# Six split slots and four raw slots for expert weights, splits up to five chunks ahead, and five smaller moves

## The chip, the cores and the metric
The kernel runs on one core of a Trainium2 chip. The metric is the device time of one execution in microseconds. TensorE (PE) multiplies; VectorE (DVE), ScalarE (ACT) and GpSimd (POOL) work beside it, and DMA queues issued by SyncE (SP) and GpSimd carry data between HBM and SBUF.

## What is computed
Two blocks on 256 tokens of width 1024: a mixer of three branches (attention, gated linear attention, mLSTM) and a feed-forward part, dense in the first block and a mixture of eight experts, two per token, in the second. All is float32.

```python
    for l in range(DEPTH):
        h = rmsnorm(x, attn_norm_g[l])
        x = x + hybrid_mixer(h, w_in[l], b_in[l], mlstm_conv_w[l], mlstm_conv_b[l], gla_gate_w[l],
                             gla_gate_b[l], gla_norm_g[l], w_up_moba[l], w_up_gla[l], w_up_mlstm[l], w_o[l])
        h = rmsnorm(x, ffn_norm_g[l])
        j = l // 2
        if l % 2 == 0:
            x = x + swiglu(h, ffn_w_gate[j], ffn_w_up[j], ffn_w_down[j])
        else:
            x = x + moe_swiglu(h, router_w[j], router_b[j], moe_w_gate[j], moe_w_up[j], moe_w_down[j])
    return rmsnorm(x, final_norm_g)
...
def swiglu(x, w_gate, w_up, w_down):
    return (jax.nn.silu(x @ w_gate) * (x @ w_up)) @ w_down
```

`DEPTH` is 2 and the hidden width 2816. In `moe_swiglu` each token goes to the two experts with the largest router logits, and their `swiglu` outputs are added with the softmax of the two logits as weights.

## The kernel before
**Chunks and splits.** Weights come in chunks of 128 x 2048 floats (1.05 MB), each as two DMA transfers of 512 KB that SyncE issues in order into a raw slot. A float32 product is made of three: the weights are split into a high part (a cast on ScalarE, `copy(hi_slot(m), slot_raw(m))`, L1359) and a low part (a subtraction on VectorE, L1795), and TensorE multiplies high by high, high by low and low by high. The low split increments `lo_ready`, on which TensorE waits for the chunk and SyncE for the raw slot that comes free. The dense stages do the same at L1286 and L1656.

**The expert stage** is a list MS of 8 x 33 = 264 steps, one chunk each; m is the number of a step. The hidden width is cut into 11 tiles i. Each has two gate/up chunks, `gu i c` with c = 0 and 1 (12 matmuls each, L1206), and a down chunk, `dn i` (12 matmuls, L1217). The order is gu 0, gu 1, dn 0, gu 2, dn 1 and so on; the first gate chunk of the next expert is put ahead of an expert's last down chunk. Between gate/up and down, ScalarE makes `silu` (L1586), VectorE the product `hid` (L2232), TensorE transposes it (two transposes, `rows_hidden_T`, L1184), ScalarE copies the high part (`yT_hi`, L1591) and VectorE makes the low part (`yT_lo`, L2245), which the down chunk needs. `next_hidden` says behind which step the transposes stand: before, tile i + 1 behind dn i.

**Slots.** `RE` raw slots hold loaded chunks, `RX` pairs of split slots hold the high and low parts. Before, RE = 8 and RX = 4, and step m splits chunk m + 3. The split waits for the raw data (`moe_in`) and for TensorE to be done with the slot (`slot_free`). The load of chunk m waits for the low split of chunk m - RE.

**Order.** Each engine has its own list in program order and nothing passes anything: what stands behind a waiting split on ScalarE or VectorE waits too.

**Other pieces.** At an expert pair's end (odd e, step dn 9) `gather` brings the next pair's rows onto partitions (L1135; `gather_hi` and `gather_lo`, L1546 and L2184, scale them). `rows_of_picks` (L2131 to L2139) makes row numbers in expert 0 at dn 4, `gates_of_picks` gates in expert 1 at dn 6, `gates_exp` (L1539, L1540) in expert 1 at dn 1 with two table loads. GpSimd stores normalised rows to HBM (L637), loads those of each pair from there (L644), stores each expert's output rows (L655) and at the end gathers each token's rows (L661) into `prow`, one set at a time, which VectorE adds (`add_picked`, L2147). At the very start the first chunks come as pieces (L860) and the third chunk, of which both halves count on one semaphore, is split whole.

## Time and profile before

| | |
|---|---|
| median of three runs | 1513.99 us (1512.26 to 1519.23) |
| the profiled execution | 1515.32 us, of it 1513.1 us in the span |
| TensorE busy | 1489.0 us, 98% of the span |
| VectorE, ScalarE, GpSimd busy | 1209.0, 957.2, 60.1 us |
| granted TensorE clock | 0.997 of full speed |
| DMA | 426.31 MB, 282 GB/s over the span |
| expert stage | about 742 us to 1501 us |

A busy TensorE here means that matmuls follow one another; one of 128 x 512 is shown as 0.39 us long, and the next starts 0.23 us after it. What can be won is the time in which it waits. A wait is put down to the instruction that released it last, and a wait on one engine reaches TensorE only if what stands behind it is late there.

### The profile page before, as it was taken

The numbers are of one execution on the slowest core, as the hardware profiler recorded it, in microseconds if no ns is written. First come the engines' busy times: TensorE is split into PE (matmuls) and PEld (weight loads), VectorE is DVE, ScalarE is ACT, GpSimd is POOL, SyncE is SP. The second block draws the span as 40 slices with busy tenths as digits, with TensorE's granted clock in tenths as the row PEclk, the third lists the DMA queues.
The fourth block names the chain that finished last, engine by engine and source line by source line (L and its number), as shares of the span: only waits on it lengthen the run. The fifth ranks groups of instructions, "written<-read, shape, count | busy, mean of one in ns | idle before, by whom it ended". The sixth has DMA issues, their size and how long they took to land.

```text
span 1513.1 us, 18975 instructions
## 1 busy us (share of the span) xinstructions
PE 1489.0 (98%) x7373; PEld 1239.7 (82%) x7373; DVE 1209.0 (80%) x1173; ACT 957.2 (63%) x907; POOL 60.1 (4%) x93
## 2 busy tenths in 40 slices
PE   9999999999999999999899999999999999999996
PEld 7898888888888898888788787888888888888885
DVE  6787976654556697976789899988889889889886
ACT  6357634544435357634787777777777777877774
POOL 2000000000000000001002000000000000000002
PEclk9999999999999999999999999999999999999998
DMA  8454555455545554556799999999999999999991
GB/s 337 182 178 144 201 180 182 176 193 195 185 177 197 181 187 148 189 190 256 296 370 401 410 405 363 391 373 383 379 367 388 386 378 370 350 390 380 380 375 58
DMA packets 117872, 426.31 MB, mean 282 GB/s; under 512 B 13392, under 2 KB 13568, under 8 KB 117776
## 3 DMA queue, kind: packets, MB, share of 16 engines
q1 hardware_dynamic: 111024, 402.44, 70.3%
q0 software_dynamic: 6464, 22.25, 4.2%
q8 instruction: 61, 1.00, 0.3%
q10 hardware_dynamic: 288, 0.34, 0.1%
q14 instruction: 35, 0.29, 0.1%
HBM read 415.01 MB, written 9.97 MB: 281 GB/s over the span
## 4 chain that ended last, share of the span: by engine, by line
PE 85%; DVE 5%; ACT 5%; issue 2%; DMA 1%; SPq 0%; DVEq 0%; ACTq 0%
PE ps L1206 29%; PE ps L750 17%; PE ps L1217 14%; PE ps L1049 8%; PE ps L740 4%; PE ps L1026 4%; PE ps L729 4%; DVE w_lo L1656 2%; PE ps L1184 1%; ACT w_hi L1286 1%; DVE w_lo L1795 1%; ACT hT_hi L1546 1%; DMA late<-dense_dram 1%; DMA prow<-y_rows,bias 1%; PE ps L708 1%
## 5 line engine op out<-in xcount | busy, mean ns | idle before, releaser
L1656 DVE TENSOR_TENSOR w_lo<-raw_m,w_hi 128x2048 fp32r<-128x2048 f32 x113 | 258.1, 2289 | 120.0 <-ACT w_hi L1286 120.0
L1286 ACT CAST w_hi<-raw_m 128x2048 fp32r<-128x2048 f32 x113 | 214.7, 1907 | 129.1 <-PE ps L750 59.2
L1795 DVE TENSOR_TENSOR w_lo<-raw_m,w_hi 128x2048 fp32r<-128x2048 f32 x99 | 226.5, 2291 | 24.4 <-ACT w_hi L1359 24.3
L1795 DVE TENSOR_TENSOR w_lo<-late,w_hi 128x2048 fp32r<-128x2048 f32 x99 | 226.4, 2290 | 22.4 <-ACT w_hi L1359 22.1
L1206 PE MATMUL ps<-w_hi,hT_hi 128*128 128x512 f32 x532 | 213.8, 402 | 1.3 <-DVE hT_lo L2184 1.3
L1206 PE MATMUL ps<-w_hi,hT_lo 128*128 128x512 f32 x532 | 208.8, 392 | 0.0
L1206 PE MATMUL ps<-w_lo,hT_hi 128*128 128x512 f32 x532 | 208.4, 392 | 0.0
L1359 ACT CAST w_hi<-raw_m 128x2048 fp32r<-128x2048 f32 x99 | 189.4, 1914 | 24.1 <-PE ps L1206 17.6
L1359 ACT CAST w_hi<-late 128x2048 fp32r<-128x2048 f32 x99 | 189.5, 1915 | 19.9 <-PE ps L1206 19.4
L750 PE MATMUL ps<-w_hi,hT_hi 128*128 128x512 f32 x464 | 183.5, 395 | 1.8 <-DVE w_lo L1656 1.8
L750 PE MATMUL ps<-w_hi,hT_lo 128*128 128x512 f32 x464 | 181.1, 390 | 0.0
L750 PE MATMUL ps<-w_lo,hT_hi 128*128 128x512 f32 x464 | 181.0, 390 | 0.0
L1795 DVE TENSOR_TENSOR w_lo_x<-late,w_hi_x 128x2048 fp32r<-128x2048 f32 x66 | 151.2, 2291 | 18.5 <-ACT w_hi_x L1359 18.4
L1359 ACT CAST w_hi_x<-late 128x2048 fp32r<-128x2048 f32 x66 | 126.4, 1915 | 11.7 <-PE ps L1206 11.7
L1206 PEld LDWEIGHTS ps<-w_hi,hT_lo 128*128 128x128 f32 x532 | 100.3, 188 | 21.3
L1206 PEld LDWEIGHTS ps<-w_hi,hT_hi 128*128 128x128 f32 x532 | 100.5, 189 | 20.2 <-DVE hT_lo L2184 1.5
L1206 PEld LDWEIGHTS ps<-w_lo,hT_hi 128*128 128x128 f32 x532 | 100.6, 189 | 19.0
L1217 PE MATMUL ps<-w_hi,yT_hi 128*128 128x512 f32 x260 | 102.6, 395 | 1.8 <-DVE yT_lo L2245 1.6
L750 PEld LDWEIGHTS ps<-w_hi,hT_hi 128*128 128x128 f32 x464 | 87.2, 188 | 20.1 <-DVE w_lo L1656 2.3
L750 PEld LDWEIGHTS ps<-w_hi,hT_lo 128*128 128x128 f32 x464 | 87.2, 188 | 18.4
L1217 PE MATMUL ps<-w_hi,yT_lo 128*128 128x512 f32 x260 | 101.6, 391 | 0.0
L1217 PE MATMUL ps<-w_lo,yT_hi 128*128 128x512 f32 x260 | 101.4, 390 | 0.0
(378 smaller groups left out, 2633.4 us busy)
## 6 DMA issues: line engine op xcount, KB each, us to landing
late<-experts_dram SPq DMA_DIRECT2D x330, 512.0 KB, 5.7
raw_m<-dense_dram SPq DMA_DIRECT2D x226, 512.0 KB, 4.0
raw_m<-experts_dram SPq DMA_DIRECT2D x198, 512.0 KB, 5.8
bias<-b_in_dram POOLq DMA_DIRECT2D x26, 256.0 KB, 5.0
y_rows<-yrow POOLq DMA_DIRECT2D x7, 512.0 KB, 7.3
x_rows<-prow POOLq DMA_DIRECT2D x6, 512.0 KB, 8.0
late<-x_rows POOLq DMA_DIRECT2D x6, 512.0 KB, 7.6
late<-dense_dram SPq DMA_DIRECT2D x4, 512.0 KB, 11.0
```

The costliest lines, as they stand in the source:

```text
L708: ins = nc.tensor.transpose(ps[:, b, (k % 2) * T + t * P:(k % 2) * T + (t + 1) * P], src[:, t, k * P:(k + 1) * P], ident[:, :])
L729: ins = mm(ps[:, b, (m % 2) * T:(m % 2 + 1) * T], wsp[a][:, s, kk * W + m * P:kk * W + (m + 1) * P], hT[r][:, k, :], start=(k == 0 and m % ...
L740: ins = mm(ps[:, b, :], yT[a][:, k, t * P:(t + 1) * P], wsp[r][:, s, k * W:(k + 1) * W], start=(k == 0 and pa == 0), stop=(k == 3 and pa = ...
L750: ins = mm(ps[:, b, :], hT[a][:, k, t * P:(t + 1) * P], wsp[r][:, s, kk * W:(kk + 1) * W], start=(k == 0 and pa == 0), stop=(k == KT - 1 a ...
L1026: ins = mm(ps[:, b, :], yT[a][:, 2 * (i % 2) + kk, t * P:(t + 1) * P], wsp[r][:, s, kk * D + h * W:kk * D + (h + 1) * W], start=(i == 0 an ...
L1049: ins = mm(ps[:, b, :], hT[a][:, k, t * P:(t + 1) * P], wsp[r][:, s, kk * W:(kk + 1) * W], start=(k == 0 and pa == 0), stop=(k == KT - 1 a ...
L1206: ins = mm(ps[:, b, :], hT[a][:, k, x * P:(x + 1) * P], w[r][:, kk * W:(kk + 1) * W], start=(k == 0 and pa == 0), stop=(k == KT - 1 and pa ...
L1217: ins = mm(ps[:, b, :], yT[a][:, y + kk, 0:P], w[r][:, kk * D + h * W:kk * D + (h + 1) * W], start=(i == 0 and kk == 0 and pa == 0), stop= ...
L1286: copy(w_hi[:, g % RS, :], slot_raw(g, False)).then_inc(hi_ready, 1)
L1359: copy(hi_slot(m), slot_raw(m, True)).then_inc(hi_ready, 1)
L1656: tt(w_lo[:, g % RS, :], slot_raw(g, False), w_hi[:, g % RS, :], ALU.subtract)\
L1795: tt(lo_slot(m), slot_raw(m, True), hi_slot(m), ALU.subtract).then_inc(lo_ready, 1)
```

## The change
It has six parts.

1. RE goes from 8 to 4 and RX from 4 to 6. The three added pairs of split slots lie where four raw slots and the fourth pair lay. `lead(m)`: step m splits chunk m + 3 up to m = 9, m + 4 from m = 10 and m + 5 from m = 20; the steps m = 10 and m = 20 split two chunks.
2. The transposes of hidden tile i stand in the middle of gate chunk gu i + 1, c = 0 (before its third row block), in place of behind dn i - 1. The first and the last tile keep theirs.
3. On VectorE the split stands behind `hid` in gu 0 and gu 10, c = 1, and behind the low half in dn 9, in place of ahead of them (before: behind `hid` in gu 0 of every expert but the first).
4. The first gather makes high and low matmuls tile by tile.
5. The third chunk of the kernel is waited for and split in halves.
6. GpSimd gathers three of the four row sets at once, into two free places and `prow`, when the last pair's rows have been taken over; VectorE adds them at dn 4, 5, 6 and 8 of the last expert (before: dn 5 to 8).

```diff
-    RM, RE, RS, RX = 3, 8, 3, 4
+    RM, RE, RS, RX = 3, 4, 3, 6
...
     def next_hidden(kind, i, c):
-        return i + 1 if kind == "dn" and i + 1 < NF else 0 if (kind, i, c) == ("gu", 1, 0) else None
+        if (kind, c) == ("gu", 0) and i:
+            return i - 1
+        return NF - 1 if (kind, i) == ("dn", NF - 2) else None
+
+    def lead(m):
+
+        return 3 + (m >= 10) + (m >= 20)
+
+    def due(m):
+
+        return range(m + lead(m - 1), min(m + lead(m) + 1, NM)) if m else range(3, 4)
...
+        w_x = over("w_x", [P, RX - RS, 2, CK], late_at + 4 * (RE - RM) * CK)
...
+        def picked(j):
+
+            return prow[:, :] if j == 2 else xs[:, j % 2 if j < 2 else 0, :]
...
+                        .then_inc(half_in if (g, h) == (RM - 1, 0) else raw_in[g % RM], 16)
...
+            b, k = FILL[(0, E - 2), "gather", 3]
+            pool.wait_ge(full[b], k + 1)
             pool.wait_ge(zero_in, 16)
             pool.wait_ge(y_out, 16 * (E - 1))
             for j in range(2 * NT):
-                if j:
-                    pool.wait_ge(rows_added, j)
-                pool.indirect_dma_start(out=prow[:, :], out_offset=None, in_=y_rows,
+                if j == 3:
+                    pool.wait_ge(rows_added, 1)
+                pool.indirect_dma_start(out=picked(j), out_offset=None, in_=y_rows,
...
+                            if (n, t, kk) == (RM - 1, 0, 2):
+                                pe.wait_ge(lo_ready, n + 1)
...
                     part(q, 0)
-                    if not first:
-                        part(q, 1)
-                if first:
-                    for q in range(4):
+                    if first:
                         pe.wait_ge(xl_ready, NT * (q // 2 + 1))
-                        part(q, 1)
+                    part(q, 1)
...
                             k = 4 * c + kk
+                            if kk == 2 and c == 0 and i > 1:
+                                rows_hidden_T(l, x, i - 1)
...
+                    if g == RM - 1:
+                        c = slice(0, CK // 2)
+                        act.wait_ge(half_in, 16)
+                        copy(w_hi[:, g, c], slot_raw(g, False)[:, c]).then_inc(piece_hi, 1)
+                        c = slice(CK // 2, CK)
+                        act.wait_ge(raw_in[g], 16)
+                        copy(w_hi[:, g, c], slot_raw(g, False)[:, c]).then_inc(hi_ready, 1)
...
-                    if m + 3 < NM:
-                        split_moe(pas, m + 3)
+                    for n in due(m):
+                        split_moe(pas, n)
...
-                    late_split = e > 0 and (kind, i, c) == ("gu", 0, 1)
+                    last_hidden = (kind, i) == ("dn", NF - 2)
+                    late_split = (kind, c) == ("gu", 1) and i in (0, NF - 1) or last_hidden
...
+                    if last_hidden:
+                        for n in due(m):
+                            split_moe(pas, n)
...
-                    if pas == 0 and (e, kind) == (E - 1, "dn") and i in (5, 6, 7, 8):
-                        add_picked(i - 5)
+                    if pas == 0 and (e, kind) == (E - 1, "dn") and i in (4, 5, 6, 8):
+                        add_picked((4, 5, 6, 8).index(i))
```

First piece: VectorE's list at m = 9 to 12 of the expert stage, before. `w_lo` and `w_lo_x` are low splits, `ytok` is `hid`, `yT_lo` the low half.

```order
L2232 TENSOR_TENSOR ytok<-ytok,ps 128x256 [waits silu_ready,bank_full1]
L1795 TENSOR_TENSOR w_lo<-late,w_hi 128x2048 [waits w_hi_ready]
L2245 TENSOR_TENSOR yT_lo<-ps,yT_hi 128x2x128 [waits hi_part_ready,bank_full2]
L1795 TENSOR_TENSOR w_lo<-late,w_hi 128x2048 [waits w_hi_ready]
L1795 TENSOR_TENSOR w_lo_x<-late,w_hi_x 128x2048 [waits w_hi_ready]
L2232 TENSOR_TENSOR ytok<-ytok,ps 128x256 [waits silu_ready,bank_full0]
```

The same place now, from `hid` of tile 3 at m = 9 on; `w_x` is an added pair, and `x2` are the two splits of m = 10.

```order
L2275 TENSOR_TENSOR ytok<-ytok,ps 128x256 [waits silu_ready,bank_full1]
L1836 TENSOR_TENSOR w_lo<-raw_m,w_hi 128x2048 [waits w_hi_ready] x2
L1836 TENSOR_TENSOR w_x<-late,w_x 128x2048 [waits w_hi_ready]
L2289 TENSOR_TENSOR yT_lo<-ps,yT_hi 128x2x128 [waits hi_part_ready,bank_full2]
L1836 TENSOR_TENSOR w_x<-raw_m,w_x 128x2048 [waits w_hi_ready]
L2275 TENSOR_TENSOR ytok<-ytok,ps 128x256 [waits silu_ready,bank_full0]
```

Between `hid` and the low half of one tile there was one split, and two stood between that low half and the next `hid`; now there are two and one, and three at m = 10.

Second piece: VectorE's list at a pair's end (expert 3, steps gu 10 c = 1 to dn 9), before. `hT_lo` are the scalings of gathered rows.

```order
L1795 TENSOR_TENSOR w_lo<-late,w_hi 128x2048 [waits w_hi_ready]
L2232 TENSOR_TENSOR ytok<-ytok,ps 128x256 [waits silu_ready,bank_full1]
L2184 SCALAR_TENSOR_TENSOR hT_lo<-ps,cols,hT_hi 128x256 [waits gathered_hi_ready,bank_full0]
...
L1795 TENSOR_TENSOR w_lo<-late,w_hi 128x2048 [waits w_hi_ready]
L2245 TENSOR_TENSOR yT_lo<-ps,yT_hi 128x2x128 [waits hi_part_ready,bank_full2]
```

The same steps now:

```order
L2275 TENSOR_TENSOR ytok<-ytok,ps 128x256 [waits silu_ready,bank_full1]
L1836 TENSOR_TENSOR w_lo<-raw_m,w_hi 128x2048 [waits w_hi_ready]
L2225 SCALAR_TENSOR_TENSOR hT_lo<-ps,cols,hT_hi 128x256 [waits gathered_hi_ready,bank_full0]
...
L2289 TENSOR_TENSOR yT_lo<-ps,yT_hi 128x2x128 [waits hi_part_ready,bank_full2]
L1836 TENSOR_TENSOR w_x<-late,w_x 128x2048 [waits w_hi_ready]
```

`hid` and the low half have each changed places with a split.

Third piece: TensorE at the transposes of a hidden tile in the first expert, before: they stand between a down chunk (L1217) and a gate chunk (L1206).

```order
L1217 MATMUL ps<-w_lo,yT_hi 128x512
L1217 MATMUL ps<-w_hi,yT_lo 128x512
L1184 MATMUL ps<-ident,ytok 128x128 [waits bank_drained2,bank_drained0]
L1184 MATMUL ps<-ident,ytok 128x128
L1206 MATMUL ps<-w_hi,hT_hi 128x512 [waits bank_drained1,w_lo_ready]
L1206 MATMUL ps<-w_lo,hT_hi 128x512
```

Now (down L1240, gate L1229, transposes L1205):

```order
L1240 MATMUL ps<-w_x,yT_lo 128x512
L1229 MATMUL ps<-w_x,hT_hi 128x512 [waits bank_drained0,w_lo_ready]
L1229 MATMUL ps<-w_x,hT_hi 128x512
L1229 MATMUL ps<-w_x,hT_lo 128x512
L1229 MATMUL ps<-w_x,hT_hi 128x512 x2
L1229 MATMUL ps<-w_x,hT_lo 128x512
L1205 MATMUL ps<-ident,ytok 128x128 [waits bank_drained2,bank_drained1]
L1205 MATMUL ps<-ident,ytok 128x128
L1229 MATMUL ps<-w_x,hT_hi 128x512 x2
```

They stand six matmuls later, inside the chunk.

## Rows read from the trace of the kernel before

**Rows 1.** The page: TensorE's busy time, and bandwidth in 40 slices of the span.
```profile
PE 1489.0 (98%) x7373; PEld 1239.7 (82%) x7373; DVE 1209.0 (80%) x1173; ACT 957.2 (63%) x907; POOL 60.1 (4%) x93
...
GB/s 337 182 178 144 201 180 182 176 193 195 185 177 197 181 187 148 189 190 256 296 370 401 410 405 363 391 373 383 379 367 388 386 378 370 350 390 380 380 375 58
```

**Rows 2.** TensorE's waits: waited for, us in total, times, longest us.
```profile
PE ps L1184 <- DVE ytok L2232: 4.7, 4, 2.1
PE ps L750 <- DVE w_lo L1656: 1.8, 1, 1.8
PE ps L1217 <- DVE yT_lo L2245: 1.6, 3, 0.5
...
PE ps L1206 <- DVE hT_lo L2184: 1.3, 1, 1.3
```

**Rows 3.** The chain that ended last, 1003 to 1018 us: start, length, what.
```profile
1004.62 2.72 PE ps L1217 x12
1007.34 0.22 PE ps L1184 x2
1007.56 5.47 PE ps L1206 x24
1013.03 2.72 PE ps L1217 x12
```

**Rows 4.** The timeline beside it: start, length, engine, line, operation, idle before.
```profile
1010.40 1.92 ACT L1359 CAST w_hi<-raw_m 128x2048 fp32r<-128x2048 f32 x1 [0.62 <-PE ps L1206]
...
1006.15 0.41 DVE L2232 TENSOR_TENSOR ytok<-ytok,ps 128x256 f32<-128x256 f32 x1
...
1009.08 0.42 DVE L2245 TENSOR_TENSOR yT_lo<-ps,yT_hi 128x256 fp32r<-128x256 f32 x1
...
1012.35 2.29 DVE L1795 TENSOR_TENSOR w_lo<-raw_m,w_hi 128x2048 fp32r<-128x2048 f32 x1 [0.25 <-ACT w_hi L1359]
```

**Rows 5.** Busy times by stretch (PE, PEld, DVE, ACT, POOL), clock, DMA share, GB/s.
```profile
1440.00:1460.00 20.00, 20.00 (x93) 16.55 (x92) 18.03 (x14) 14.77 (x13) 0.00 (x0) 1.00 1.02 401
```

**Rows 6.** Half-chunk loads (L527) issued at 746.9:747.6, 1000:1100 and 797:860.
```profile
DMA to landing us min/median/max: 3.2/3.7/4.1
...
DMA to landing us min/median/max: 3.6/5.4/7.6
...
DMA to landing us min/median/max: 5.5/11.4/13.8
```

**Rows 7.** The same for the third chunk's first half (L494), issued at 3.67.
```profile
DMA to landing us min/median/max: 9.8/9.8/9.8
```

**Rows 8.** Timeline of the third chunk's split.
```profile
14.76 1.91 ACT L1286 CAST w_hi<-late 128x2048 fp32r<-128x2048 f32 x1 [0.61 <-DMA late<-dense_dram]
...
16.69 2.29 DVE L1656 TENSOR_TENSOR w_lo<-late,w_hi 128x2048 fp32r<-128x2048 f32 x1 [1.64 <-ACT w_hi L1286]
```

**Rows 9.** VectorE's timeline at a pair's end, the scalings of gathered rows.
```profile
927.75 3.22 DVE L2184 SCALAR_TENSOR_TENSOR hT_lo<-ps,cols,hT_hi 128x256 fp32r<-128x256 f32 x8
```

**Rows 10.** The chain near the end.
```profile
1464.11 9.26 DMA prow<-y_rows,bias
...
1473.39 1.28 DVE xt L2147
```

**Rows 11.** VectorE's timeline, first and last of the nine row-number operations.
```profile
793.43 0.18 DVE L2131 TENSOR_TENSOR bias<-bias 128x32 f32<-128x32 f32 x1
...
794.68 0.17 DVE L2139 TENSOR_SCALAR bias<-bias 128x4 uint32<-128x4 f32 x1
```

**Rows 12.** ScalarE's timeline, first and last of four instructions with the table loads.
```profile
856.85 1.28 ACT L1539 ACT_TABLE_LOAD   x1
...
859.66 0.20 ACT L1540 ACTIVATE st<-ones 128x2 f32<-128x2 f32 x1
```

**Rows 13.** GpSimd's timeline: the first of four row stores, the first pair's loads.
```profile
795.71 2.26 POOL L637 DMA_INDIRECT x_rows<-late,bias  x1 [86.97 <-DVE bias L2139]
...
813.40 1.14 POOL L644 DMA_DIRECT2D late<-x_rows  x2 [7.96 <-DMA x_rows<-late,bias]
```

More of the change, by code:

```diff
@@ L129, in program @@
     NM = E * FFC
-    assert len(MS) == NM and NM % RE == 0 and NM % RX == 0 and RX == RS + 1
+    assert len(MS) == NM and NM % RE == 0 and NM % RX == 0 and RE - RM + 2 * (RX - RS) == 7
     def ends_pair(e, kind, i):
@@ L136, in next_hidden @@
     def next_hidden(kind, i, c):
-        return i + 1 if kind == "dn" and i + 1 < NF else 0 if (kind, i, c) == ("gu", 1, 0) else None
+        if (kind, c) == ("gu", 0) and i:
[5 more added lines that the diff above has]
+        return range(m + lead(m - 1), min(m + lead(m) + 1, NM)) if m else range(3, 4)
+    assert [n for m in range(NM) for n in due(m)] == list(range(3, NM))
     def by_rows(pas, e):
@@ L258, in program @@
         xn_lo = over("xn_lo", [P, NT, D], tmp_at)
-        w_hi_x = over("w_hi_x", [P, CK], late_at + 4 * (RE - RM) * CK)
-        w_lo_x = over("w_lo_x", [P, CK], late_at + 4 * (RE - RM + 1) * CK)
+        w_x = over("w_x", [P, RX - RS, 2, CK], late_at + 4 * (RE - RM) * CK)
         xs = late[:, 7 * CK:8 * CK].rearrange("p (t n) -> p t n", t=NT)
@@ L372, in hi_slot @@
         def hi_slot(m):
-            return w_hi[:, m % RX, :] if m % RX < RS else w_hi_x[:, :]
+            return w_hi[:, m % RX, :] if m % RX < RS else w_x[:, m % RX - RS, 0, :]
         def lo_slot(m):
-            return w_lo[:, m % RX, :] if m % RX < RS else w_lo_x[:, :]
+            return w_lo[:, m % RX, :] if m % RX < RS else w_x[:, m % RX - RS, 1, :]
         ps = ctx.enter_context(nc.psum_tensor("ps", [P, 8, W], f32))
@@ L406, in program @@
         picks_ready = sem("row_numbers_ready")
-        rows_in = sem("picked_rows_in")
+        rows_in = [sem(f"picked_rows_in{i}") for i in range(2 * NT)]
         rows_added = sem("picked_rows_added")
@@ L720, in chunk @@
                         await_drained(l, left, i)
-                pe.wait_ge(lo_ready, n + 1)
+                if n == RM - 1:
+                    pe.wait_ge(piece_lo, KT - 1)
+                else:
+                    pe.wait_ge(lo_ready, n + 1)
                 if name in FEATURE_MAJOR:
@@ L1231, in moe_pass @@
                     ih = next_hidden(kind, i, c)
-                    if ih is not None and (e, ih) != (E - 1, NF - 1):
+                    if ih == 0 or ih == NF - 1 and e < E - 1:
                         rows_hidden_T(l, x, ih)
@@ L1282, in split_to @@
                     g = nsplit[0]
-                    act.wait_ge(raw_in[g % RM], 32 * (g // RM + (g % RM > 1)))
+                    if g == RM - 1:
[5 more added lines that the diff above has]
+                        copy(w_hi[:, g, c], slot_raw(g, False)[:, c]).then_inc(hi_ready, 1)
+                        nsplit[0] += 1
+                        continue
+                    act.wait_ge(raw_in[g % RM], 32 * (g // RM + (g % RM > 1)) - 16 * (g % RM == RM - 1))
                     if g >= RS:
@@ L1654, in split_to @@
                     g = nsplit[0]
+                    if g == RM - 1:
+                        c = slice(0, CK // 2)
+                        dve.wait_ge(piece_hi, KT - 1)
+                        tt(w_lo[:, g, c], slot_raw(g, False)[:, c], w_hi[:, g, c], ALU.subtract).then_inc(piece_lo, 1)
+                        c = slice(CK // 2, CK)
+                        dve.wait_ge(hi_ready, g + 1)
+                        tt(w_lo[:, g, c], slot_raw(g, False)[:, c], w_hi[:, g, c], ALU.subtract).then_inc(lo_ready, 1)
+                        nsplit[0] += 1
+                        continue
                     dve.wait_ge(hi_ready, g + 1)
@@ L2141, in add_picked @@
             def add_picked(j):
[L2143 removed]
+                dve.wait_ge(rows_in[j], 16)
                 if j:
@@ L2214, in moe_pass @@
                         many = dve.value_load(cnt_i[0:1, 0:1], min_val=0, max_val=T)
-                    late_split = e > 0 and (kind, i, c) == ("gu", 0, 1)
+                    last_hidden = (kind, i) == ("dn", NF - 2)
+                    late_split = (kind, c) == ("gu", 1) and i in (0, NF - 1) or last_hidden
                     if ends_pair(e, kind, i):
                         gather_lo(pas, e + 1)
-                    if m + 3 < NM and not late_split:
-                        split_moe(pas, m + 3)
+                    if not late_split:
+                        for n in due(m):
+                            split_moe(pas, n)
                     if (kind, i) == ("dn", NF - 1) and not by_rows(pas, e):
@@ L2233, in moe_pass @@
                         if late_split:
-                            split_moe(pas, m + 3)
+                            for n in due(m):
+                                split_moe(pas, n)
                         if e and i == 1 and not by_rows(pas, e - 1):
@@ L2246, in moe_pass @@
                            yT_hi[:, r, 0:P], ALU.subtract).then_inc(drained[b], 1)
+                    if last_hidden:
+                        for n in due(m):
+                            split_moe(pas, n)
                     if pas == 0 and (e, kind, i) == (0, "dn", 4):
```

9 lines of the change are left out of this document (5 added, 4 removed).

## The prediction
> **What bounds the kernel now.** I read the page first: TensorE is busy 98% of the span, and the slices show only where the DMA queues are near full: 360 to 410 GB/s through the expert stage, from 750 us to the end [rows 1]. So nothing can be won but the gaps of TensorE. The list of waits of TensorE gives them: 4.7 us for `hid` (four waits), 1.8 us for the third chunk, 1.6 us for the low half of the transposed hidden rows (three waits), 1.3 us for the first gathered rows [rows 2]. Then the chain in order of time for one steady hidden tile: 5.47 us for two gate/up chunks, 2.72 us for a down chunk, 0.22 us for two transposes, 8.41 us for three chunks, or 2.80 us a chunk [rows 3]. Beside it I lay ScalarE and VectorE in the same stretch [rows 4], and last the loads: how long one takes from issue to landing, alone and in traffic [rows 5, 6].
>
> I count in the profiled execution, 1515.3 us (span 1513.1 and 2.2 around it), and carry the sum over to the median, 1514.0.
>
> **Gains.** (a) The third chunk. Its first half lands 9.8 us after its issue at 3.67 us, so at 13.5 [rows 7]; today its 1.91 us cast starts at 14.76 and its 2.29 us subtraction at 16.69 [rows 8], and TensorE waits 1.84 us. As halves, the cast (0.95) starts when ScalarE is free of the eighth piece, about 14.15, the subtraction (1.15) ends near 16.4, before TensorE asks (about 17.0); the second half is 1.2 us behind, and TensorE has 1.4 us of work on the first. The whole wait goes, and some 0.2 us of hand-over: **-2.0** (-1.3 to -2.1). The list of waits has nothing else for a chunk of weights up to the expert stage, so I let it pass to the end.
>
> (b) The first gather, tile by tile instead of all high and then all low. TensorE's 1.3 us wait for `hT_lo` goes, since the first two tiles are then done 1 us earlier. But VectorE has four splits in a row behind it, and the low half of the first hidden tile can't come sooner than they do; half stays: **-0.7** (0 to -1.3).
>
> (c) Pair ends. The low half of the last hidden tile stands behind a 2.29 us split today and then in front of it (second piece of the order, above). That is the 1.6 us of three waits [rows 2], 2.1 us with the hand-overs. But eight scalings of gathered rows, 3.22 us [rows 9], now start behind one more split, and the first gate chunk of the next expert needs four of them. I take half back: **-1.2** (0 to -2.1).
>
> (d) The end. VectorE waits for a gathered row set (9.26 us of DMA on the chain), `hid` stands behind it, and TensorE loses 2.1 of the 4.7 us there [rows 10, 2]. Early gathers end that. The four additions of 1.28 us stay, three in successive tiles: a tile has 8.41 us and VectorE's list is 3 x 2.29 + 0.42 + 0.41 = 7.70, so each tile with an addition is 0.57 too long, 1.5 us in all with what the order adds. **-0.8** (-2.3 to 0).
>
> **Costs of the new order.** Now the transposes stand in the middle of the next gate chunk (third piece). Let that chunk start at 0 (1007.56 in the chain): half of 5.47 is 2.74, the transposes stand at 1.4, the down chunk begins at 2.74 + 0.22 + 2.74 = 5.7, less 0.2 by which a matmul is issued ahead of the end of the last. ScalarE's cast starts 0.1 after the slot comes free (1010.40, where the chunk before ended at 1010.30) and takes 1.92; VectorE's split runs from 2.05 to 4.34, the low half behind it to 4.7 [rows 4]. Spare before the down chunk: about **0.7 us**, where the order before leaves the same step over 3 us (1009.50 to 1013.03). `hid` has gained: it is ready 0.8 us ahead of the transposes today (1006.56 and 1007.34), and they now come 1.4 later. VectorE's own idle time ahead of that step is 0.3 more. So whatever holds up VectorE by more than 1.0 us just before it is paid by TensorE.
> (e) Two steps split two chunks, at m = 10 and m = 20 (first piece). 2.29 - 1.0 = 1.3 each, and the first meets ScalarE's 0.7 us row stores: **+3.0** (0 to +4.6; nothing, if VectorE has run ahead by then).
> (f) Nine small operations that make row numbers take 793.43 to 794.85, 1.4 us [rows 11], and a like group in the second expert 1.6: 0.4 and 0.6 beyond the spare, less the 0.3 that the second costs today: **+0.7** (-0.3 to +1.5).
> (g) Two table loads keep ScalarE from 856.85 to 859.86 [rows 12]. Of the 4.7 us that wait for `hid`, 2.1 are the one at the end, and I put about 1.6 of the rest on these loads; 3.0 - 1.0 = 2.0 then: **+0.4** (-1.6 to +1).
>
> **The ring of raw slots.** The four slots are the term that decides. A load is issued when the split of the chunk that many places ahead ends. The round is issue, landing, cast 1.91, subtraction 2.29 and hand-overs, 4.3 us after landing. With eight slots the round has 8 x 2.80 = 22.4 us; with four 11.2, so landing may take 6.9 us, and 0.7 more before TensorE feels it. What it takes: a chunk is two transfers, the second issued 0.4 later. Alone 4.1 + 0.4 = 4.5 us; between 1000 and 1100 us the half takes 5.4 in the median and 7.6 at most, so 5.8 and 8.0 a chunk [rows 6]. Spare at the median 1.1, with the 0.7 1.8; at the worst less than none.
>
> Bandwidth itself is there: 401 GB/s in a stretch where the queue was full [rows 5], so 2.6 us for 1.05 MB against 2.80. The Trainium skill (SBUF — State Buffer, The DMA setup-cost knee) says that a core's HBM gives about 358 GB/s, which would make the stage DMA-bound before and after; the trace's 401 GB/s disagrees, and I go by the trace.
>
> Extra traffic is what a short ring can't hide. Row stores and pair loads from 795.71 to about 823 are six transfers of 0.5 MB, 7.8 us [rows 13]: in 28 us, ten chunks (25.7) and 7.8 are 5.5 too much. The eight-slot ring shows it as landings of 11.4 in the median and 13.8 at most [rows 6] and hides it. With four: 5.5 less 1.8 and less about 2.3 that TensorE has lost to (e) and (f) in that stretch, +1.4 (0 to +5). Two later pair loads with an expert's rows, 1.5 MB or 3.9 us each over 20 us with 1.4 of room: 2.5 less 1.8, +0.6 each. Single row stores, 1.3 us, fit. The three gathers that (d) issues together, with the store ahead of them, are 2 MB or 5.2 us in 14 us with 1 of room: 4.2 less 1.8, +2.4 (0 to +4). **+5.0** (0 to +12).
>
> Sum: -2.0 - 0.7 - 1.2 - 0.8 + 3.0 + 0.7 + 0.4 + 5.0 = **+4.4**, 1519.7 in the profiled frame and **1518** at the median. Before and after are within 0.5% of each other; that, 7.6 us, is about what a measurement of this kernel can tell from no change.
>
> **Rivals.**
> - *The ring binds.* If chunks land in more than 6.9 us on the average, TensorE follows the ring: each 0.1 us above costs 0.025 us a chunk, 6.6 us over 264. For it: 8.0 us is seen without extra traffic. Against: the median is 5.8, and a ring that lags issues later and finds the queue emptier. At 7.1 us it adds 13: **1531**. It decides from 6.9 us on.
> - *Loads land as if alone*, 4.5 us. Spare 2.4 + 0.7 = 3.1: the ring costs 0.1 at the row stores, 1.1 at the end, 0 between: 1.2 in place of 5.0, **1515**. For it: fewer loads in flight. Against: the 5.4 us median came with hardly more of them. The Trainium skill (DMA: Bandwidth & Descriptors, Anatomy of one DMA) gives about 2.0 us plus bytes at 436 GB/s, an estimate of 4.4 us for a chunk: the trace agrees for the lone load alone.
> - *The lead covers it.* Splits five ahead leave TensorE chunks for 14 us, so it might run through all of (e) and most of the ring's delays: -4.7 + 0.7 + 0.4 and +1 for the rest, -2.6; with what I held back in (b) to (d), another -3.0, **1508**. Against: TensorE never waits for a split in this stage today; it waits for `hid` and the low half, which stand behind splits in VectorE's list, and the lead moves neither.
> - *The change does nothing in the steady part*: the three-chunk period stays 8.41 us in all four cases but the first rival; that is part of the forecast.
>
> **Chances.** Forecast 0.40, ring binds 0.22, as if alone 0.20, covered 0.18. Slower by over 0.5% (above 1521.6): the ring case and a quarter of the forecast, 0.32. Faster (under 1506.4): a good half of the last, 0.10. Within: 0.58. The range goes from just under the covered case, 1506, to 1536, past the ring case's figure; beyond lie a mean landing over 7.2 us on the one side and all gains at their ends on the other, 1 in 10 each.
>
> **What would show it.** The wait for the third chunk gone, its matmuls from about 17.0. Waits of TensorE for the low half (the down chunk's line) grown from 1.6 to 5 us or more, for `hid` down to under 2. New idle time of ScalarE before its cast, ended by a DMA: some 5 to 15 us in total in 800 to 835, at pair ends and after 1410; if it stands throughout, at every chunk, the ring binds; if there is none, the loads land as if alone. Landings in 1000 to 1100 at 4.5 to 5.8 us a chunk. Wrong would be: a period of more than 8.45 us in the quiet stretches, or waits of TensorE for a split itself.

## The result, and the profile after

The changed kernel takes **1538.3 us** at the median (1536.6 to 1540.4), the kernel before 1513.7 in the same comparison: a ratio of 1.0155, 95% interval 1.0141 to 1.0169. It is slower by 1.55%. The forecast was 1518 with a range of 1506 to 1536, so the time lies just outside it. The outcome that I held likeliest (within 0.5% of before, 0.58) did not come either. Three executions in the experiments lasted far longer than the others of their kernels (8562, 2502 and 1855 us) and are left out of the medians below; with the second of them the run with a lead of three would stand at 1539.7 us, the figure that the expectations use, in place of 1535.8. The profiled execution took 1538.1 us, with a span of 1536.2.

TensorE's waits, with the same columns as [rows 2]. The gate/up line is now L1229, the down line L1240, the transposes L1205:

```profile
PE ps L1240 <- DVE yT_lo L2289: 22.1, 19, 4.9
...
PE ps L1205 <- DVE ytok L2275: 0.7, 2, 0.4
```

The waits that I wanted gone are gone (`hid` 4.7 to 0.7, the first gathered rows 1.3 to none), and the wait for the low half has grown from 1.6 to 22.1 us. (Of the 23.1 us that the span grew, 15.0 are idle time of TensorE and 8.1 busy time, 1489.0 to 1497.1. Part of the 8.1 is a lower clock, at the end of this text, and about 0.16 us behind each stop, where the next matmul follows later than the bracket says: the stop of 4.90 below costs 5.06. The rest is not explained.) Behind it stands a wait that the kernel before does not have. These are ScalarE's groups for the expert splits: busy time and mean, idle time before, and what ended it:

```profile
L1391 ACT CAST w_hi<-raw_m 128x2048 fp32r<-128x2048 f32 x110 | 210.3, 1912 | 72.1 <-DMA raw_m<-experts_dram 40.4 <-PE ps L1229 16.8 <-PE ps L1240 8.1
L1391 ACT CAST w_x<-raw_m 128x2048 fp32r<-128x2048 f32 x88 | 168.5, 1916 | 46.0 <-DMA raw_m<-experts_dram 23.4 <-PE ps L1240 14.7 <-PE ps L1229 7.9
L1391 ACT CAST w_x<-late 128x2048 fp32r<-128x2048 f32 x44 | 84.2, 1913 | 23.6 <-DMA late<-experts_dram 13.8 <-PE ps L1229 9.7
L1391 ACT CAST w_hi<-late 128x2048 fp32r<-128x2048 f32 x22 | 42.1, 1915 | 14.6 <-DMA late<-experts_dram 10.1 <-PE ps L1240 4.4
```

ScalarE waits 88 us for loads, at 99 of its 264 expert splits and in every part of the stage (21 us of it between 1100 and 1200 us); before, at none. The prediction had said 5 to 15 us in three places. The chain that ended last puts 11% of the span on DMA:

```profile
PE 69%; DMA 11%; DVE 9%; ACT 7%; issue 3%; SPq 1%; POOL 0%; DVEq 0%; ACTq 0%; POOLq 0%
```

**How a late load reaches TensorE.** The longest stop, read from below: TensorE, then VectorE, then ScalarE. The idle time before an operation and what ended it stand in brackets.

```profile
812.22 1.22 PE L1240 MATMUL ps<-w_x,yT_hi 128*128 128x512 f32 x2 [4.90 <-DVE yT_lo L2289]
```
```profile
809.53 2.29 DVE L1836 TENSOR_TENSOR w_lo<-raw_m,w_hi 128x2048 fp32r<-128x2048 f32 x1 [2.93 <-ACT w_hi L1391]
811.75 0.42 DVE L2289 TENSOR_TENSOR yT_lo<-ps,yT_hi 128x256 fp32r<-128x256 f32 x1
```
```profile
807.61 1.90 ACT L1391 CAST w_hi<-raw_m 128x2048 fp32r<-128x2048 f32 x1 [3.33 <-DMA raw_m<-experts_dram]
809.41 0.36 ACT L1623 CAST yT_hi<-ps 128x256 fp32r<-128x256 f32 x1
```

The chunk that TensorE needs at 807 had been split by 800.7. But the high and low half of its hidden rows stand behind the split of a later chunk, and that split waits for its load. The list of an engine is in order, so a late load holds up everything after it.

**Where the time went.** I took the start of every expert chunk's matmuls from TensorE's timeline and subtracted the kernel before. (The last line, 263, is the last chunk.) A level stretch means that nothing is lost in it against the kernel before. (The two columns on the right belong to runs below, the one with eight raw slots and the one with a window of five.)

```
chunk     after   eight slots   window of five
  0       -3.4        -3.4          -3.3
 12       -3.2        -3.3          -3.1
 24       +9.3        -3.0          -2.9
 36      +11.8        -3.0          +1.5
 72      +12.6        -3.1          +1.5
108      +15.1        -3.0          +1.5
156      +18.7        -3.5          +1.1
192      +19.3        -3.5          +1.1
240      +22.3        -3.9          +0.6
252      +26.0        -3.5          +3.0
263      +22.2        -7.1          -0.5
```

The gains ahead of the expert stage came in full. Then 15 us go between chunks 12 and 36 (775 to 845 us), another 14 in some ten small steps up to chunk 252, and 3.7 come back at the end. Between the steps the tile has its old length, 8.41 us, as in [rows 3]:

```profile
1381.91 4.11 PE ps L1229 x18
1386.02 2.72 PE ps L1240 x12
1388.74 1.36 PE ps L1229 x6
1390.10 0.22 PE ps L1205 x2
1390.32 4.11 PE ps L1229 x18
```

### The profile page after: what moved, and what is told of

It reads as the page before. It is cut to its first block, busy times and chain, and to the rows that moved or that the text cites. A ratio compares the mean times of both kernels' runs of the same rounds, so it can differ in the third digit from the quotient of the medians.

```text
span 1536.2 us, 18977 instructions
## 1 busy us (share of the span) xinstructions
PE 1497.1 (97%) x7373; PEld 1238.6 (81%) x7373; DVE 1207.0 (79%) x1174; ACT 958.7 (62%) x908; POOL 59.3 (4%) x93
## 4 chain that ended last, share of the span: by engine, by line
PE 69%; DMA 11%; DVE 9%; ACT 7%; issue 3%; SPq 1%; POOL 0%; DVEq 0%; ACTq 0%; POOLq 0%
PE ps L1229 18%; PE ps L774 16%; PE ps L1240 11%; PE ps L1073 8%; DMA raw_m<-experts_dram 5%; DMA late<-experts_dram 5%; PE ps L762 4%; PE ps L1050 4%; PE ps L751 4%; DVE w_lo L1836 2%; DVE w_x L1836 2%; ACT w_hi L1391 2%; ACT w_x L1391 1%; DVE w_lo L1697 1%; ACT w_hi L1318 1%
## 5 line engine op out<-in xcount | busy, mean ns | idle before, releaser
L1836 DVE TENSOR_TENSOR w_x<-raw_m,w_x 128x2048 fp32r<-128x2048 f32 x88 | 200.9, 2290 | 25.1 <-ACT w_x L1391 24.9
L1229 PE MATMUL ps<-w_x,hT_hi 128*128 128x512 f32 x696 | 218.6, 395 | 0.3
L1391 ACT CAST w_x<-raw_m 128x2048 fp32r<-128x2048 f32 x88 | 168.5, 1916 | 46.0 <-DMA raw_m<-experts_dram 23.4
L1229 PEld LDWEIGHTS ps<-w_x,hT_hi 128*128 128x128 f32 x696 | 127.5, 188 | 25.8 <-issue 0.9
L1229 PE MATMUL ps<-w_hi,hT_hi 128*128 128x512 f32 x356 | 142.6, 401 | 0.0
L1229 PE MATMUL ps<-w_hi,hT_lo 128*128 128x512 f32 x356 | 139.2, 391 | 0.0
L1229 PE MATMUL ps<-w_lo,hT_hi 128*128 128x512 f32 x356 | 138.9, 390 | 0.0
L1229 PE MATMUL ps<-w_x,hT_lo 128*128 128x512 f32 x348 | 136.1, 391 | 0.0
L1240 PE MATMUL ps<-w_x,yT_hi 128*128 128x512 f32 x360 | 115.3, 402 | 11.2 <-DVE yT_lo L2289 11.1
L1836 DVE TENSOR_TENSOR w_x<-late,w_x 128x2048 fp32r<-128x2048 f32 x44 | 100.7, 2289 | 14.5 <-ACT w_x L1391 14.5
L774 PEld LDWEIGHTS ps<-w_hi,hT_hi 128*128 128x128 f32 x464 | 87.1, 188 | 18.5 <-DVE w_lo L1697 0.5
L774 PEld LDWEIGHTS ps<-w_hi,hT_lo 128*128 128x128 f32 x464 | 87.1, 188 | 18.5
L1391 ACT CAST w_x<-late 128x2048 fp32r<-128x2048 f32 x44 | 84.2, 1913 | 23.6 <-DMA late<-experts_dram 13.8
L1240 PEld LDWEIGHTS ps<-w_x,yT_hi 128*128 128x128 f32 x360 | 66.8, 191 | 31.3 <-DVE yT_lo L2289 18.4
```

The source lines that it names most:

```text
L774: ins = mm(ps[:, b, :], hT[a][:, k, t * P:(t + 1) * P], wsp[r][:, s, kk * W:(kk + 1) * W], start=(k == 0 and pa == 0), stop=(k == KT - 1 a ...
L1229: ins = mm(ps[:, b, :], hT[a][:, k, x * P:(x + 1) * P], w[r][:, kk * W:(kk + 1) * W], start=(k == 0 and pa == 0), stop=(k == KT - 1 and pa ...
L1240: ins = mm(ps[:, b, :], yT[a][:, y + kk, 0:P], w[r][:, kk * D + h * W:kk * D + (h + 1) * W], start=(i == 0 and kk == 0 and pa == 0), stop= ...
L1391: copy(hi_slot(m), slot_raw(m, True)).then_inc(hi_ready, 1)
L1836: tt(lo_slot(m), slot_raw(m, True), hi_slot(m), ALU.subtract).then_inc(lo_ready, 1)
```

## Experiments

The theory after the first look: the ring of four raw slots costs nearly all of it. Rivals: the lead of splits (two steps that split two chunks); the traffic beside the chunks; the poor start of the stage; the place of the low half behind the split. All runs are compared with the kernel before on their own chip (1513.9 to 1514.7 us there).

### Ring and lead, one at a time

Eight slots and a lead of three, which leaves only the other parts of the change:

```
-    RM, RE, RS, RX = 3, 4, 3, 6
+    RM, RE, RS, RX = 3, 8, 3, 4
...
-        return 3 + (m >= 10) + (m >= 20)
+        return 3
```


> The changed kernel with eight raw slots, four split slots and the splits three chunks ahead: the other five parts of the change alone. Ring theory (the four raw slots cost the time): all of the loss goes, the gains of the five parts stay: 1507 to 1512 us, ScalarE waits for no expert load, TensorE's waits for the low half under 5 us. Lead theory (the two steps with a double split and what stands behind them cost it): the same, since this kernel has no double step either; the next kernels part the two. Order theory (the transposes inside the gate chunk leave the low half too little room): stays above 1525, with waits for the low half of 15 us or more.

Measured 1508.84 us, ratio 0.9964 (0.9949 to 0.9979). This is faster than before.

Only the lead set back to three (RE = 4, RX = 6 stay). The expectation's ring theory has 1528 to 1534:

> The changed kernel (four raw slots, six split slots) with the splits three chunks ahead throughout, so no double steps. Lead theory: the stalls at the two double steps (3.1 and 5.1 us, and what follows from them) go and the time falls to 1515 or below. Ring theory: the raw slots still come free four chunks behind, the stage still begins four chunks poorer and the row stores still delay the loads; only the two chunks that the longer lead had to gain are saved, some 5 us: 1528 to 1534.

Measured 1535.8 us (1534.1 to 1543.6; ratio on record 1.0166, 1.0124 to 1.0208, and 1.0139 by the medians). This is just above the ring theory's band and far from the lead theory's. Removing the lead saves 2.5 us at the median, which three runs that spread over 10 us can't tell from nothing. Four slots against eight cost **27 us**.

Six slots (RE = 6, RX = 4) with a lead of three:

> Six raw slots, four split slots, splits three ahead; all else as in the changed kernel. Ring theory: a load may take 5.6 us longer than with four, 12.5 us a chunk; only the landings of the row stores' stretch are longer, so 1507 to 1514, with a small stall between 800 and 840 us. Lead theory: as with eight slots, the same within noise.

Measured 1510.3 us, ratio 0.9975 (0.9965 to 0.9985). Two slots fewer cost 1.5 us, the next two 25.5.

The changed kernel with half of the bytes:

```
-                    for h in range(2):
+                    for h in range(1):
...
-                act.wait_ge(moe_in[m % RE], 32 * ((pas * NM + m) // RE + 1))
+                act.wait_ge(moe_in[m % RE], 16 * ((pas * NM + m) // RE + 1))
```


> The changed kernel as it is, but of each expert chunk only the first of its two transfers is loaded (the second half of the slot holds old data, so the output is another): the DMA load of the stage is halved, the instructions of the three engines are the same. Ring theory: chunks land in about 3.5 to 4.5 us, ScalarE's waits for loads vanish, the time falls by some 20 us to 1512 to 1518; what is left of the stalls at the double steps (about 1.3 us each) and behind the table loads is the cost of the order. Lead or order theory: the time stays above 1525.

Measured 1511.5 us, ratio 0.9979 (0.9969 to 0.9990), just under the band of the ring theory. With the same four slots, order and lead, but loads that land sooner, 26.8 us of the 1538.3 go. What is dear is a short ring together with the time that a load takes.

The same with a lead of three, which prices the double steps alone:

> The changed kernel with a lead of three throughout, and only the first half of each expert chunk loaded (the second half is left out). Against the run with half loads and the lead of 3 to 5 (1511.57 us, stops of 1.70 at 776.5 and 0.92, 0.34 and 0.81 at 804 to 822) it prices the two steps that split two chunks, with the loads out of the way. Theory, these steps cost 3 to 4 us: 1507.5 to 1509 us, no stop over 0.5 us between 770 and 830. Rival, what the half loads leave of the loss comes from the ring and not from the double steps: 1511 to 1513 us.

Measured 1508.4 us, ratio 0.9961 (0.9950 to 0.9972): **3.1 us** for the double steps (2.7 by the two ratios, since the runs were on different chips; 4.3 by the chunk starts of the two traces, from chunk 12 to 36). The stops at 778, 805 and 823 us in the run before (1.54, 0.76 and 0.65 us) are absent here.

### By place

Half loads for the first 40 chunks only, or from chunk 40 on only; the edit is the one above with `range(1 + (m >= 40))` or `range(1 + (m < 40))` and the waits counted to match.

> The changed kernel; of the first 40 expert chunks only the first half is loaded (the second half of each is left out, the splits still take the whole slot). TensorE's chunk starts in the changed kernel fall 12.0 us behind from chunk 0 to 36 and with half loads throughout only 4.8. Theory, losses add up by place: the start of the stage gives back 10 to 11 us, the rest stays, 1526 to 1530 us. Rival, the ring recovers by itself and the time lost at the start would else be saved later: under 1518 or over 1533 us.

Measured 1527.0 us, ratio 1.0098 (1.0071 to 1.0125): 11.3 less than the changed kernel.

> The changed kernel; of the expert chunks from number 40 on only the first half is loaded (the second half of each is left out). Same theory of places: the start's loss stays and the 16 us lost after chunk 40 go, 1520 to 1524 us. Rival, the later losses follow from the lateness of the start: as the second run, it would then come out near 1530.

Measured 1521.8 us, ratio 1.0047 (1.0030 to 1.0064): 16.5 less. 11.3 and 16.5 make 27.8, and half loads throughout gave 26.8. The losses add up by place; the later ones do not follow from the lateness of the start.

### The ring in the old order

```
-    RM, RE, RS, RX = 3, 8, 3, 4
+    RM, RE, RS, RX = 3, 4, 3, 4
```


> The kernel before with one number changed: four raw slots in place of eight, its old order and four slots for split chunks. The ring of four costs 30 us at the median in the new order with a lead of three (1539.7 against 1508.8 with eight slots). Theory A, the ring is dear wherever the transfers of 1.05 MB per 2.8 us have to come through four slots, and what stands in front of the low half matters little: 1538 to 1546 us. Theory B, the ring is dear only because the new order leaves 0.7 us of spare between a split and the low half of the hidden rows, where the old one leaves over 3 us: 1518 to 1528 us, with waits of TensorE for hid and the low half together under 15 us.

Measured 1531.9 us, ratio 1.0124 (1.0107 to 1.0141): 18 us, between the two theories. TensorE's waits in the profiled execution, the fastest of five (1525.9 us):

```profile
PE ps L1184 <- DVE ytok L2232: 12.7, 12, 3.0
...
PE ps L1217 <- DVE yT_lo L2245: 1.6, 3, 0.5
```

The old order shields the low half (1.6 us, as before), and now `hid` pays, 12.7 in place of 4.7. So the ring costs 18 us in the old order and 27 in the new one: the spare ahead of the low half matters, but it is the smaller part.

### The traffic of the row stores

```
-                    pool.indirect_dma_start(out=x_rows, out_offset=bass.IndirectOffsetOnAxis(ap=row_x[:, j:j + 1], axis=0),
-                                            in_=xs[:, t, :], in_offset=None).then_inc(x_stored, 16)
-            pool.wait_ge(x_stored, 16 * 2 * NT)
```


> The changed kernel without the four stores of normalised rows (2 MB between 797 and 807 us; the pair loads behind them come that much earlier, and experts 2 to 7 compute on zeroed rows). Theory, what a ring of four can't hide is traffic beside the expert chunks: the stop of 5.06 us at 806.9 us and part of those at 822.9 and 832.0 go, 5 to 7 us less, 1531 to 1534 us. Rival, the start of the stage is short of loaded chunks whatever else moves: the stop shrinks by under 2 us, 1536 to 1539 us.

Measured 1536.5 us, ratio 1.0140 (1.0110 to 1.0169), in the rival's band. The 5 to 7 us that my theory promised are not there. The stop is as long as with the stores:

```profile
813.51 1.22 PE L1240 MATMUL ps<-w_x,yT_hi 128*128 128x512 f32 x2 [5.37 <-DVE yT_lo L2289]
```

The ring is in arrears before the row stores would come. From chunk 6 to 24 ScalarE's casts start 2.96 us apart in this run (TensorE needs 2.80), and 14 of the 19 start 0.02 us after their load has landed.

But this run does not show that other traffic is harmless. Without the stores the two pair loads of 0.5 MB moved up, from 815.69 to 797.43 us, and land at 803.4 and 806.8. The chunk whose split the stop waits for was issued between, at 799.1, and was complete at 808.9:

```profile
797.43 1.09 POOL L661 DMA_DIRECT2D late<-x_rows  x2 [90.41 <-DVE bias L2180]
```
```profile
DMA to landing us min/median/max: 6.8/8.1/9.4
```

A run without the pair loads too would have to tell; there is none.

### The place of the hidden rows

`hid` and both halves of the hidden rows ahead of the split in every gate/up step, on ScalarE and VectorE. ScalarE's part; VectorE's is alike:

```
+                    hidden_first = kind == "gu" or (kind, i) == ("dn", NF - 2)
-                    for n in due(m):
+                    for n in due(m) if not hidden_first else ():
                         split_moe(pas, n)
...
+                    for n in due(m) if hidden_first else ():
+                        split_moe(pas, n)
```


> The changed kernel (four raw slots, six for split chunks, lead 3 to 5) with one thing moved: in each gate/up step the product hid and the high and low half of the hidden rows stand ahead of the split on ScalarE and VectorE, so that a split that waits for its load holds back only splits. In the changed kernel all 22 us of waits for the low half stand behind such a split, at times when the chunk that TensorE needs had been split 3 to 5 chunks ahead. Theory, the lead of splits can cover the late loads (14 us at a lead of five, 8 at three) as soon as TensorE's other operands don't queue behind them: 1510 to 1520 us, waits for the low half under 5 us. Rival, four slots can't carry 1.05 MB per 2.80 us at the start of the stage (2.96 us a chunk from chunk 6 to 24 in the run without row stores), so the lead is used up and TensorE then waits for the splits themselves: 1528 to 1540 us.

Measured 1532.6 us, ratio 1.0125 (1.0103 to 1.0146). The time is in the rival's band, but by a way that neither text names:

```profile
PE ps L1240 <- DVE yT_lo L2289: 11.9, 13, 3.2
PE ps L1229 <- DVE hT_lo L2228: 5.0, 3, 1.9
PE ps L1205 <- DVE ytok L2278: 4.1, 1, 4.1
```

TensorE still doesn't wait for a split. It waits for `hid` and the low half, which now stand behind the split of the step before. Moved by one place, the block is the same. The move gained 5.7 us of the 1538.3. A lead measured in chunks does not cover a late load while the splits share a list with what TensorE needs next.

The same move with eight slots and a lead of three:

> The version with eight raw slots, four for split chunks and a lead of three (1508.84 us), with the same move. Its trace has three stops of TensorE for the low half left, 1.04 us at 750.1, 1.91 at 861.4 (two table loads ahead of the splits) and 0.53 at 905.5. Theory, they go: 1505 to 1507 us. Rival, the split of the next chunk comes up to 2 us later and takes VectorE past the product hid or holds up the slot of the chunk after: the same time or slower, 1508 to 1514 us.

Measured 1510.2 us, ratio 0.9974 (0.9964 to 0.9983): the rival holds. The stop at chunk 4 went, the one at 43 shrank from 1.75 to 1.36, but TensorE waited 1.5 us for the gathered rows at each of three pair ends.

### A rich start, and the missing slot

Eight slots, of which the loads use four from chunk 10 on; and a window of five from the start. With w = 4 from m = 10, or w = 5 from m = 5, the line is:

```
+                        sp.wait_ge(lo_ready, MOE_BASE + pas * NM + m - w + 1)
```


> The version with eight raw slots and a lead of three (1508.84 us); from chunk 10 on a load waits for the split of the chunk four places ahead, as if there were four slots, so the expert stage starts with ten chunks issued or landed as before the change, and only then runs on four. With four slots from the start and the same lead the time is 1539.7 us, of which TensorE's chunk starts show 7.6 us lost from chunk 12 to 36. Theory, this loss is the poor start (six chunks loaded and no DMA from 728.6 to 744.1 us): 1529 to 1533 us, under 2 us lost between chunks 12 and 36. Rival, four slots are too few around 800 us however the stage starts, since the row numbers, the row stores and the pair loads come there: 1536 to 1541 us.

Measured 1531.0 us, ratio 1.0104 (1.0088 to 1.0121). The median is in the theory's band, but the trace does not bear it out. From chunk 12 to 36 it loses 7.4 us, as the run with four slots from the start does (7.6), in one stop of 4.05 beside the row stores and the slow matmuls behind it:

```profile
814.84 0.79 PE L1242 MATMUL ps<-w_hi,yT_hi 128*128 128x512 f32 x1 [4.05 <-DVE yT_lo L2291]
```

The two profiled executions are 1534.1 and 1534.5 us; the medians, 4.8 us apart, come from four and three runs that spread over 5 and 10 us. I can't settle what the rich start is worth. It does not shield chunks 24 to 36 when the lead is three.

> The same version with the load of every chunk from number 5 on waiting for the split of the chunk five places ahead, a ring of five. Six slots cost 1.5 us against eight, four cost 30.9. By the sum of the prediction a slot more lets a chunk take 2.80 us longer from issue to landing, 9.7 us in place of 6.9, over all landings but those beside the row stores (9.8 to 13.2 us). Theory, the price is a knee at four: 1509 to 1514 us. Rival, it falls evenly from four to six: 1518 to 1526 us.

Measured 1514.2 us, ratio 1.0001 (0.9990 to 1.0013). This is the theory's knee, 0.2 us above its upper edge: against eight slots, six cost 1.5 us, five 5.4 and four 27.0. The loss of the five is where the sum of the prediction had put that of four. Two stops follow the row stores, one of 1.39 stands by the gathers at the end, and the only others behind chunk 12 are the two that eight slots have too, 1.75 (the table loads) and 0.36 (right column of the table):

```profile
813.11 0.50 PE L1242 MATMUL ps<-w_hi,yT_hi 128*128 128x512 f32 x1 [2.01 <-DVE yT_lo L2291]
...
823.62 0.50 PE L1242 MATMUL ps<-w_hi,yT_hi 128*128 128x512 f32 x1 [1.78 <-DVE yT_lo L2291]
```

### A version faster than before and after

Eight slots, a lead of three, and the hidden rows first only up to chunk 59, ahead of the first pair end (`hidden_first = (kind == "gu" and m < 60) or ...`).

> The version with eight raw slots and a lead of three, and hid and the hidden rows ahead of the split only in the gate/up steps up to chunk 59, where its three stops lie (1.04, 1.91, 0.53 us). With the move everywhere, the stop at chunk 4 went, the one at 43 shrank to 1.52, and three of 1.7 us came before the experts 2, 4 and 6. Theory, without those three: 1507.0 to 1508.5 us. Rival, the move costs elsewhere too: 1509 to 1511 us.

Measured **1507.1 us**, ratio 0.9950 (0.9934 to 0.9967). In the expert stage one stop of 1.35 us (the table loads) is the longest left. The 1.7 us against the version without the move (1508.84) are not clear of noise: the two were on different chips, and the intervals of their ratios overlap.

## Why the prediction was wrong, step by step

**The step that failed is the landing time in the ring's sum, and with it the rule that an average under the limit is safe.** The prediction said "the half takes 5.4 in the median and 7.6 at most, so 5.8 and 8.0 a chunk". The 5.4 is the median over both halves of all chunks [rows 6]. A chunk is complete when its second half lands, and that one comes later. For the chunk issued at 1046.14 and 1046.51 in the kernel before (these two loads alone; minimum, median, maximum):

```profile
DMA to landing us min/median/max: 5.6/6.2/6.9
```

The first half took 5.6, the second 6.9, the chunk 0.37 + 6.9 = 7.2, where "median plus 0.4" would say 6.6. Over the 36 chunks issued from 1000 to 1100 us in that trace I get a median of 6.55 and an upper quartile of 7.07. So the limit of 6.9 was not 1.1 above the median but 0.35, and 12 of the 36 chunks were over it before anything was changed. The rival "the ring binds" decides at 6.9; what I read as far from it was next to it.

The right median alone would not have given the loss. The changed kernel, for its halves in the same stretch:

```profile
DMA to landing us min/median/max: 3.1/5.2/7.9
```

Taken per chunk that is a mean of 6.40 us, with 15 of 35 over 6.9. The mean stays under the limit, where the prediction's rule has the ring cost nothing, and TensorE is late all the same: the single chunks over the limit count, not their average.

**What follows from that, and was missing.** At a disturbance, what counts is how fast the ring recovers. A chunk takes 2.6 us of DMA by my own sum and 2.80 of TensorE, so the transfers win back 0.2 us a chunk; and as soon as a split waits for its load, every free slot is a load in flight, and the loads queue behind each other. I wrote that "a ring that lags issues later and finds the queue emptier". The chain of the changed kernel shows the ring going round in a stretch without other traffic:

```profile
1066.55 0.33 SPq L544
1066.88 0.04 issue
1066.92 7.18 DMA late<-experts_dram
...
1074.12 1.92 ACT w_hi L1391
...
1076.07 2.30 DVE w_lo L1836
...
1078.38 0.33 SPq L544
...
1089.78 0.33 SPq L544
...
1101.39 0.33 SPq L544
```

Three rounds take 11.8, 11.4 and 11.6 us, four chunks each, against the 11.2 that TensorE needs. That is 1.2 us lost over the three, and chunk 108 starts 1.1 us later against the kernel before than chunk 102 does. After it the tile is 8.41 us again. So the ring binds now and then, and loses 0.3 to 3 us each time and 5 us beside the row stores, where I had let it bind always, or only beside other traffic. By the half loads it costs 26.8 us in place of +5.0, and by the slots, with a lead of three, 27. The half loads themselves took this long from 1000 to 1100 us:

```profile
DMA to landing us min/median/max: 3.1/3.2/5.0
```

The Trainium skill (DMA: Bandwidth & Descriptors, Anatomy of one DMA) gives, for transfers that GpSimd issues, 2.0 us plus bytes at 436 GB/s, an estimate of 3.2 us for the 0.52 MB of a half. Here, with SyncE's loads, the trace agrees with it: 3.2 us in the median, with one half for every 2.80 us. With two halves in that time the median is 5.2 to 5.4.

**The start of the stage.** I costed the row stores and had nothing for what stands ahead of them. With four slots no load can be issued from 723 until the first split of the stage is done. The stretch from 730 to 744 us, before and then after (length, PE, PE loads, DVE, ACT, POOL busy, granted clock, DMA share, GB/s):

```profile
730.00:744.00 14.00, 10.84 (x82) 8.67 (x83) 10.46 (x36) 9.14 (x18) 0.00 (x0) 1.00 0.61 244
```
```profile
730.00:744.00 14.00, 13.22 (x90) 10.97 (x91) 11.17 (x32) 11.09 (x18) 0.00 (x0) 1.00 0.01 2
```

The stage begins with six chunks loaded, not ten, and two steps then ask for two chunks more than TensorE uses. That those two steps and the ring together make the 15 us up to chunk 36 is what the runs suggest: with a lead of three the ring alone loses 7.6 there, with half loads and the full lead the loss is 4.7. The sum is 12.3; the rest is not separated. Nor is the poor start's own share: with ten chunks loaded, a lead of three and four slots the same chunks lose 7.4.

**The other terms**, by chunk starts of the run with eight slots, unless said otherwise:

- (a) third chunk, -2.0: -2.1. (b) first gather, -0.7: -1.3, the whole wait. VectorE's splits behind it held nothing back.
- (c) pair ends, -1.2: -1.4 in three steps (0.5, 0.4, 0.5).
- (d) the end, -0.8: **-3.5**. The stop of 2.1 us went, and with it the slow matmuls behind it (below), which I had not seen; and the 1.5 us that I charged for the additions did not come. The chain there is TensorE alone.
- (e) double steps, +3.0: +3.1 between the medians of the two half-load runs, 4.3 between their traces.
- (f) +0.7: +0.3. (g) +0.4: +0.5; the stop behind the table loads is 1.75 us.
- "Against" the rival of the covering lead I had written that TensorE waits for what stands behind splits, and the lead moves neither. The run with the hidden rows first confirms it.

So of the terms other than the ring only (d) left its bounds (-2.3 to 0), on the good side; without ring and lead the change is worth 5.9 us at the median (I had 3.6). The one term that decides was out by over 20 us, and its bounds (0 to +12) by over 14. My sign that "the ring binds" would show as a tile of over 8.45 us in quiet stretches was also wrong: it never did.

## What to carry to other kernels

Size a ring by the landing of whole items (the last transfer of each) and by the late ones, not by the median transfer. In this kernel the upper quartile, 7.1 us, and the 4.3 us of work on the slot make 11.4 us; over four slots that is 2.85 us, above TensorE's 2.80, and over five 2.3. Five slots still cost 5.4 us, most of it beside the row stores, so other traffic wants a sixth. This is drawn from one kernel. Where the queue's own margin is a few per cent, as the 2.6 to 2.80 us here, nothing lost is won back soon, and one slot, 4 to 5, was worth 22 us, more than any reordering here. And a lead of work does not decouple an engine if what is needed next stands behind it in the same list.

## What the runs showed of the hardware

TensorE's clock fell behind some of its stops. Here is the changed kernel after a stop of 2.89 us: the matmul of 128x512, 0.39 us long at full clock, takes 0.63 for a while.

```profile
776.67 0.39 PE L1229 MATMUL ps<-w_hi,hT_lo 128*128 128x512 f32 x1
779.95 0.80 PE L1240 MATMUL ps<-w_hi,yT_hi 128*128 128x512 f32 x1 [2.89 <-DVE yT_lo L2289]
780.54 0.63 PE L1240 MATMUL ps<-w_lo,yT_hi 128*128 128x512 f32 x1
...
782.68 0.63 PE L1240 MATMUL ps<-w_hi,yT_hi 128*128 128x512 f32 x1
783.10 0.43 PE L1240 MATMUL ps<-w_lo,yT_hi 128*128 128x512 f32 x1
783.37 0.39 PE L1240 MATMUL ps<-w_hi,yT_lo 128*128 128x512 f32 x1
```

The granted clock of that stretch and of the one behind the stop of 4.90 us (columns as above) is 0.50, the lower of the clock's two levels, 1.2 GHz in place of 2.4:

```profile
780.00:783.00 3.00, 3.00 (x7) 2.42 (x8) 2.46 (x3) 2.55 (x3) 0.00 (x0) 0.50 1.03 385
...
812.00:816.00 4.00, 3.78 (x9) 3.01 (x10) 1.63 (x2) 2.18 (x2) 0.31 (x1) 0.50 1.02 418
```

The price is 1.2 us behind the first stop and 2.0 behind the second (0.2 for each matmul that came at the lower clock, 6 and 10 of them), 3.2 in the run. In the expert stages of all runs of this study it stands behind stops of 2.06 us or more, and nowhere else. In the kernel before it stands behind the stop of 2.13 us near the end, at a cost of 1.4 us:

```profile
1480.00:1483.00 3.00, 3.00 (x9) 2.33 (x8) 3.00 (x3) 2.11 (x2) 0.00 (x0) 0.51 0.12 46
```

The run with a window of five had stops of 2.01 and 1.78 us and no matmul at the lower clock behind them. Nor does every longer stop have it: behind the third long stop of the changed kernel, 2.78 us, ending at 1457.40, the clock stayed at full speed, and so it did behind one of 3.14 us in the run with half loads from chunk 40 on.

```profile
1457.00:1460.00 3.00, 2.60 (x11) 2.15 (x12) 2.43 (x3) 2.63 (x3) 0.00 (x0) 1.00 1.02 397
```

Outside the expert stage it fell once without such a stop: in the profiled execution of the run with half loads and a lead of three (1511.8 us, its median being 1508.4), at 600 us, behind a wait of 0.56 us.

```profile
600.00:607.00 7.00, 6.55 (x33) 5.42 (x34) 6.43 (x10) 3.05 (x3) 0.54 (x1) 0.53 0.80 310
```

So a stop of TensorE of over 2 us can cost 1 to 3 us more than its length, and need not.
